# Quarter-array scores, a moved right side and later loads in a two-block kernel

## What is computed

```python
def hybrid_mixer(h, ...):
    p = jnp.einsum('bsd,de->bse', h, w_in)
    ...
    y_c = rwkv7_bidir(...)                     # the recurrence, both directions
    branch = jnp.einsum('bsnc,ncd->bsnd', ys, w_branch)
    gates = jax.nn.sigmoid(gl + b_gate)
    merged = jnp.sum(gates * branch, axis=2)
    return jnp.einsum('bsd,de->bse', merged, w_out)
...
# one step of the recurrence, 8 heads of width 64, both directions
sa = einsum('bhij,bhj->bhi', state, -kk_t)
state = state * w_t + sa * (kk_t * a_t) + v_t * k_t
y_t = einsum('bhij,bhj->bhi', state, r_t)
...
# a layer of the first block
x = layer_norm(alpha * x + mix, ln1_g[l], ln1_b[l])
hid = jnp.square(jax.nn.relu(x @ w_up[l]))
x = layer_norm(alpha * x + hid @ w_down[l], ln2_g[l], ln2_b[l])
```

## Time and profile before

| | us |
|---|---|
| median of 3 runs (2545.81 to 2548.17) | 2546.51 |
| the profiled execution | 2546.9 |
| its span, first to last instruction | 2545.1 |
| TensorE busy | 2476.9 |
| VectorE busy | 1440.0 |
| ScalarE busy | 524.4 |
| GpSimd busy | 319.5 |

### The profile page before, as it was taken

One profiled execution on the slowest core, in us unless ns is written; L12 is line 12 of the kernel. 1 busy time (PEld: TensorE's weight loads), 2 busy tenths in 40 slices (PEclk: granted clock), 3 DMA queues, 4 the chain that ended last, 5 costly groups with the idle time before them and its releaser, 6 DMA issues. The chain is left out here.

```text
span 2545.1 us, 40375 instructions
## 1 busy us (share of the span) xinstructions
PE 2476.9 (97%) x16928; PEld 1891.9 (74%) x16928; DVE 1440.0 (57%) x2688; ACT 524.4 (21%) x1233; POOL 319.5 (13%) x367
## 2 busy tenths in 40 slices
PE   8999999999999999999999999999999999999998
PEld 7887786854788778685477747888886666666997
DVE  1576655855157665563357735555334488854775
ACT  1342220100134221010014910000003243411000
POOL 2002102210100220221000000000000155410110
PEclk9999999999999999999999999999999999999999
DMA  8332125887434112597631022322222534334553
GB/s 269 116 116 69 53 85 188 297 293 246 141 117 125 59 53 85 188 301 285 241 123 67 2 67 71 95 83 75 91 87 69 165 100 134 122 104 145 167 173 108
DMA packets 253611, 341.93 MB, mean 134 GB/s; under 512 B 7252, under 2 KB 179412, under 8 KB 253304
## 3 DMA queue, kind: packets, MB, share of 16 engines
q1 hardware_dynamic: 241632, 311.71, 37.6%
q10 hardware_dynamic: 8920, 17.67, 2.2%
q0 software_dynamic: 2880, 9.96, 1.1%
HBM read 338.13 MB, written 1.19 MB: 133 GB/s over the span
## 5 line engine op out<-in xcount | busy, mean ns | idle before, releaser
L1159 PE MATMUL PS<-MEM 128*128 128x256 f32 (+1 forms) x2632 | 447.9, 332 | 2.6 <-ACT MEM L1616 1.2
L1159 PEld LDWEIGHTS PS<-MEM 128*128 128x128 f32 x2632 | 406.3, 190 | 43.8 <-issue 1.9
L415 PE MATMUL PS<-MEM 128*128 128x256 f32 x1632 | 356.8, 379 | 1.1 <-DMA MEM<-w_up 1.1
L1575 ACT ACTIVATE MEM<-PS 128x256 f32<-128x256 f32 (+3 forms) x389 | 158.8, 439 | 923.7 <-PE PS L415 223.0
L415 PEld LDWEIGHTS PS<-MEM 128*128 128x128 f32 x1632 | 308.3, 190 | 44.7 <-DMA MEM<-w_up 2.3
L470 PE MATMUL PS<-MEM 128*128 128x512 f32 x608 | 265.3, 597 | 10.9 <-DMA MEM<-w_down 6.0
L2194 DVE SCALAR_TENSOR_TENSOR MEM<-MEM 128x512 f32<-128x512 f32 x280 | 216.4, 805 | 62.7 <-DMA MEM<-ada_w 57.2
L470 PEld LDWEIGHTS PS<-MEM 128*128 128x128 f32 x608 | 115.3, 191 | 156.9 <-issue 141.5
L3139 POOL TENSOR_TENSOR MEM<-MEM 128x1 f32<-128x1 f32 (+1 forms) x34 | 21.6, 636 | 1270.3 <-DVE MEM L2140 812.8
L704 PE MATMUL PS<-MEM 128*128 128x256 f32 x768 | 180.8, 386 | 0.0
L1472 PE MATMUL PS<-MEM 128*128 128x512 f32 (+1 forms) x512 | 171.6, 488 | 0.0
(11 more groups left out here) (400 smaller groups left out, 3283.6 us busy)
## 6 DMA issues: line engine op xcount, KB each, us to landing
MEM<-w_in SPq DMA_DIRECT2D x54, 1024.0 KB, 5.4
MEM<-ada_w SPq DMA_DIRECT2D x48, 1024.0 KB, 7.3
MEM<-w_up SPq DMA_DIRECT2D x32, 1024.0 KB, 5.6
MEM<-w_down SPq DMA_DIRECT2D x32, 1024.0 KB, 5.1
MEM<-ssm_w_in SPq DMA_DIRECT2D x24, 1024.0 KB, 5.5
MEM<-ffn_gate SPq DMA_DIRECT2D x22, 1024.0 KB, 5.3
MEM<-ffn_up SPq DMA_DIRECT2D x22, 1024.0 KB, 5.3
MEM<-ffn_down SPq DMA_DIRECT2D x20, 1024.0 KB, 5.1
```

The source lines that it names most:

```text
L415: ins = pe.matmul(bank[:, 0:T], W[:, k, c * P:(c + 1) * P], XT[:, k, :], start=k == 0, stop=k == KT - 1)
L1159: ins = pe.matmul(out, left[:, k, :], right[:, k, :], start=k == 0, stop=k == 3)
L1575: act.activation(out, view(b), func, **kw).then_inc(S("bank_read_by_act"), 1)
```

## The change

It has five parts.

1. In `scores` each matmul of 128 output partitions becomes two of 64, so that each runs on one 64x64 quarter of the array. There are 16 calls a layer: 8 matmuls each in place of 4.
2. `right_first` moves from level 3 (behind its filler slot) to level 4 (before its filler slot), `right_second` from behind level 3's `level_xt` to behind level 4's filler slot. ScalarE's copy of `rh` moves along. `keys_flipped` of the next pair moves from before level 5's filler slot to behind it, and ScalarE's copy of it too.
3. In the filler's table the slot of level 2's `level_z` gets one matmul in pairs 0 and 1 (none before), and the slot `W` of pair 3 gets three (four before).
4. The waits ahead of `w_out` and `w_down` are taken out. In `wide` a wait ahead of each slab of the first half asks for as many tiles as have been used by its end: of `gated` for `w_out`, of `hid_squared` for `w_down`.
5. In layer 1 the context rows are loaded by SyncE's queue right behind the fourth slab of `w_down`'s first half, once the up products are done. ScalarE issues the five constants behind its work on the context rows at the middle of `w_down`.

```diff
@@ -57,9 +57,9 @@
 
-FILL_SLOT = {"mask": (4, 0, 0, 0), "begin": (12, 0, 0, 0), ("z", 1): (3,) * 4, ("z", 2): (0, 0, 3, 3), ("z", 3): (3,) * 4, ("z", 4): (3,) * 4, ("z", 5): (3,) * 4,
+FILL_SLOT = {"mask": (4, 0, 0, 0), "begin": (12, 0, 0, 0), ("z", 1): (3,) * 4, ("z", 2): (1, 1, 3, 3), ("z", 3): (3,) * 4, ("z", 4): (3,) * 4, ("z", 5): (3,) * 4,
              ("x", 1): (0,) * 4, ("x", 2): (0,) * 4, ("x", 3): (0,) * 4, ("x", 4): (0,) * 4, ("x", 5): (2,) * 4,
-             "W": (3, 3, 3, 4), "XO": (2, 2, 2, 4), "sa": (2, 2, 2, 4)}
+             "W": (3, 3, 3, 3), "XO": (2, 2, 2, 4), "sa": (2, 2, 2, 4)}
 
@@ -437,7 +437,7 @@
 
-            def wide(w, src, nk, keyf, nt=NT, between=None, second=None, by_token=False, midway=None, turn=None):
+            def wide(w, src, nk, keyf, nt=NT, between=None, second=None, by_token=False, midway=None, turn=None, ready=None, beside=None):
 
@@ -450,6 +450,10 @@
                         W = b_slab(w, k0, 512 * half, n)
+                        if half == 0 and s == 3 and beside:
+                            beside()
+                        if half == 0 and ready:
+                            pe.wait_ge(S(ready[0]), ready[1] + k0 + n)
                         last = k0 + n == nk
@@ -792,7 +796,8 @@
                             rhs = KR[pb:pb + 64, d, ct, c, :, :].rearrange("p a b -> p (a b)")
-                            ins = pe.matmul(banks[half][:, 256 * j:256 * j + 256], BK[pb:pb + 64, d, ct, c, part, :], rhs, start=True, stop=True)
+                            for o in (0, HB):
+                                ins = pe.matmul(banks[half][o:o + HB, 256 * j:256 * j + 256], BK[pb:pb + 64, d, ct, c, part, o:o + HB], rhs, start=True, stop=True)
                             if j == 1:
@@ -1034,12 +1039,14 @@
                                 keys_turned(g)
+                        if m == 4:
+                            right_first(gs)
+                        slot(pair, ("z", m))
+                        if m == 4:
+                            right_second(gs)
                         if m == LEVELS - 1:
...
                                 keys_flipped(g)
-                        slot(pair, ("z", m))
-                        if m == 3:
-                            right_first(gs)
                         if m == LEVELS - 1:
@@ -1048,8 +1055,6 @@
                             scores(gs[m - 1], 1)
-                        if m == 3:
-                            right_second(gs)
                         if m in (3, 4) and follow:
@@ -1080,8 +1085,7 @@
                     pass
-                pe.wait_ge(S("merged"), l + 1)
-                wide(w_out[l], lambda k, t: MRG[:, k, t * P:(t + 1) * P], KT, lambda h, t: ("wo", l, h, t), by_token=True, turn=n0 + 1)
+                wide(w_out[l], lambda k, t: MRG[:, k, t * P:(t + 1) * P], KT, lambda h, t: ("wo", l, h, t), by_token=True, turn=n0 + 1, ready=("gated", 24 * l + 16))
                 later = turn_banks(n0 + 1, 1)
@@ -1109,9 +1113,10 @@
                     channels(w_up[l], 256 * s, 256, [("up", l, 2 * s), ("up", l, 2 * s + 1)], ("act", "act"))
-                pe.wait_ge(S("hid_squared"), (DFF // P) * (l + 1))
+                up_done = len(hist)
                 wide(w_down[l], lambda k, t: HID[:, k, t * P:(t + 1) * P], DFF // P, lambda h, t: ("dn", l, h, t), between=True, by_token=True,
-                     midway=(lambda: turn_normed(0, (1,))) if l == DEPTH - 1 else None, turn=n0 + 2 if l < DEPTH - 1 else None)
+                     midway=(lambda: turn_normed(0, (1,))) if l == DEPTH - 1 else None, turn=n0 + 2 if l < DEPTH - 1 else None,
+                     ready=("hid_squared", DFF // P * l), beside=(lambda: ctx_at.append((len(slabs) - 1, up_done))) if l == DEPTH - 1 else None)
                 ada_turned(ADA_DOWN + ADA_UP)
@@ -1782,10 +1787,10 @@
                                 copy(("bkt", l, g), flat(BKT[g % 2][:, :, :]))
+                        slot(("z", m))
                         if m == LEVELS - 1 and pair < 3:
                             flipped((2 * pair + 2, 2 * pair + 3))
-                        slot(("z", m))
-                        if m == 3:
+                        if m == 4:
                             for g in gs:
@@ -1811,16 +1816,16 @@
                 if l == DEPTH - 1:
+                    squares2(0, (2, 3))
+                copy(("modrow", first), AROW, lambda b: b[:, 0:256])
+                if l == DEPTH - 1:
+                    act.wait_ge(S("x_gained"), NT * (2 * l + 2))
+                    modulated(0, (1,))
                     act.dma_start(ROT[:, :], io["rot"]).then_inc(S("const2_loaded"), 16)
...
                     act.dma_start(DIAG[:, :, :], io["diag"]).then_inc(S("const2_loaded"), 16)
-                    squares2(0, (2, 3))
-                copy(("modrow", first), AROW, lambda b: b[:, 0:256])
-                if l == DEPTH - 1:
-                    act.wait_ge(S("x_gained"), NT * (2 * l + 2))
-                    modulated(0, (1,))
                     squares2(0, (0,))
@@ -3190,7 +3195,6 @@
                 else:
-                    pool.dma_start(CTOK[:, :, :], io["ctx"].rearrange("b (t p) d -> p (b t) d", p=P)).then_inc(S("ctx_loaded"), 16)
                     for t in RMS_TILES[0][:NT]:
@@ -3268,6 +3272,9 @@
                 sp.dma_start(dst, src).then_inc(S(f"slab_loaded{s % NSLOT}"), 16)
+                if s == ctx_at[0][0]:
+                    sp.wait_ge(S("bank_filled"), ctx_at[0][1])
+                    sp.dma_start(CTOK[:, :, :], io["ctx"].rearrange("b (t p) d -> p (b t) d", p=P)).then_inc(S("ctx_loaded"), 16)
 
```

More of the change, by code:

```diff
@@ L349, in build @@
         NARROW_BANK = {"p1": 0, "p6": 1, "p7": 1, "p5": 2, "p4": 3, "p2": 4, "p3": 5}
-        narrow_at = []
+        narrow_at, ctx_at = [], []
         seven_at = []
```

## The result

The changed kernel takes 2529.65 us (median of 4 runs, 2526.40 to 2532.14), the kernel before 2546.50 beside it: 0.9932 of its time, 95% interval 0.9915 to 0.9949. So it is faster, by 16.9 us and not by 29.5, and lies 2.7 us above the forecast range. The profiled execution took 2527.41 with a span of 2525.6, that is 19.5 less than before's.

A forecast was written before the change was run, and what follows sets the result against it. TensorE, busy 97% of the span, was taken as the bound; 17.8 + 2.4 + 1.3 + 6.3 + 1.7 = 29.5 us off 2546.9 gave 2517.4, median 2517.0, range 2508.5 to 2527.

The forecast's parts named there:

- Scores as quarters: Recurrence's scores calls: four quarters run at once, so a call takes 0.90 instead of 1.21 us, 0.31 saved.
- Where the 0.31 counts: Recurrence, level by level: which calls shorten the path, with order and filler gains; 8.9 us a layer, 17.8 for two.
- The order: Recurrence, pairs 0 to 2: moved right sides save 2.8 us a layer; level 4 to 5 with flipped keys 3.5.
- The sum itself: Recurrence, per layer: level 1, level 2, levels 3 and 4, level 4 to 5, pair 3, slot W; given as 8.9.
- Z3 to X4: Recurrence, from Z of level 3 to X of level 4: 8.42 us shrinks to 7.5, 0.9 saved, three times.
- One more dip, 1.7: Layer 1's pair 3: 3.4 us at clock 0.50 expected to go with less idle time, saving 1.7 us.
- `w_out`, 2.4: Start of `w_out`: the wait of 1.2 us a layer goes, saving 2.4 us.
- `w_down`, layer 0: 0: Start wait of 1.84 us goes but comes back whole at the third slab; 0 saved, 1.8 as other bound.
- `w_down`, layer 1: 1.3 + 6.3: Start wait goes, 1.3 us; third slab's wait behind `ctx` and constants goes, 4.6, with a clock dip, 1.7.
- Quarters gain nothing: Rival on the scores: both forms fill the array, so 9 calls a layer lose 0.31 each; + 5.6, 2522.6; chance 0.12.
- The clock rival: Pair 3's dip stays and layer 0's `w_down` wait brings one of its own; + 3.4, 2520.4; chance 0.12.
- The prediction's own test: Recurrence pairs: the prediction is wrong if they shorten by less than 6 us a layer.

The follow-up runs named there:

- e1: Changed kernel with the scores written in one step over 128 rows again, not as quarters; 2528.31 us, 0.9929 of the kernel before.
- e5: Changed kernel with each 1 MB weight slab loaded during the recurrence sent as four 256 KB transfers; 2523.99 us, 0.9919 of the kernel before.
- e6: Changed kernel with scores in one step over 128 rows and the recurrence's slabs in four transfers; 2524.46 us, 0.9918 of the kernel before.
- e2: Kernel before with the scores as quarters alone; 2550.18 us, 1.0016 of the kernel before.
- e3: Kernel before with only the waits per slab in w_out and w_down and the later loads of context rows and constants; 2540.16 us, 0.9973.
- e14: Changed kernel with 32 one-column matmuls (half a block of instructions) ahead of the first projection; 2526.06 us, 0.9925 of the kernel before.
- e4: Changed kernel with 64 one-column matmuls (256 instructions, one whole block) ahead of the first projection; 2533.50 us, 0.9949 of the kernel before.
- e7: Changed kernel with each slab loaded during the recurrence sent whole and then once more; 2535.18 us, 0.9960 of the kernel before.

## Why the prediction was off

The direction and most mechanisms were right, the size was not. In the profiled execution 19.5 us came of 29.5. Of the 10.0 that are missing, 12.2 are in the recurrences (17.8 and 1.7 forecast, 7.3 found) and 1.5 in layer 1's `w_down`; 1.0 and 2.7 came where nothing was forecast. The median is 2.6 further off, for it lies 2.2 above the profiled execution and not 0.4 below. The 12.2 in turn are 8.0 us of added pauses, 1.7 for the dip that stayed, and 2.5 more.

- **Scores as quarters, "Where the 0.31 counts".** The failed step. The 0.31 a call was right (0.87 for the predicted 0.90). The sum took it for granted that TensorE always has its next instruction, and costed the doubled records at nothing beside the array's time. The quarters' share of the 17.8 was, by the prediction's own rival, 5.6 us: it came to nothing (e1, e5 against e6), and in the kernel before to a loss (e2). Between the pauses 3.4 to 4.4 of it are there, but the added pauses are 6.8 (against e1) and 8.0 (e5 against e6). The other 1 to 2 us may be calls that run into VectorE sooner, as the 0.17 at L908 shows; this is not measured.
- **The order** (right sides, flipped keys, filler): the other 12.2 of the 17.8. e1 is 11.8 us faster than e3, so this was right. Z3 to X4 took 7.57 for 7.5.
- **The sum itself.** 0.6 + 1.2 + 2.8 + 3.5 + 0.3 + 0.4 is 8.8 and not 8.9. This changes nothing that matters.
- **One more dip, 1.7.** Wrong: there is still one in the second recurrence, behind another pause. It is gone in e5. That pauses make it is likely and not shown (see below).
- **`w_out`, 2.4.** Right, 2.4 in the trace.
- **`w_down`, layer 0: 0.** 1.0 in the trace. The third slab took back 2.0, for the predicted 1.8, and a later slab was waited for 1.0 less.
- **`w_down`, layer 1: 1.3 + 6.3.** 6.1 in the trace. Of the wait for the third slab 1.34 us stayed, with the modelled end 1.5: too large by that. The clock is full there, as said.
- **The 2.7 elsewhere** are not the change's, as far as I can tell: 1.7 of it is a dip at 2250.7 that before's trace has and this one has not, and most of the rest shorter waits for `w_up` (1.1 us before, 0.3 after). That is luck of the profiled execution.
- **The rivals.** "Quarters gain nothing" was given 0.12, with 2522.6 and another reason (that both forms fill the array). Its effect came, its reason did not. The clock rival, 0.12, came by half: one dip stayed, layer 0's `w_down` has none. No case held two at once. A case in which the recurrence's instructions run short was missing, though 2.2 us of "issue" stood in the list of waits that the earlier trace rows is cut from.

The prediction's own test, pairs that shorten by less than 6 us a layer, has come true against it: 4.2 and 3.1.

## What to carry to other kernels

Count instructions as well as microseconds when a matmul is cut into smaller ones. An estimate from these traces: the 300 instructions in hand must last some 2 us until a packet starts and 2.5 until it can be used, 4.5 together. A stretch that uses them up much faster will wait, and what is saved in it can come back as pauses. Idle time put down to "issue" on a busy engine may be such a wait; see whether it stands 256 records apart. Large transfers that are not urgent are better sent in pieces in such a stretch (6.8 us here), and small matmuls kept for the places where they shorten the path.

## What the hardware showed

- TensorE's instructions come in packets of 16 KB. In the recurrences a packet starts in the mean some 2 us after record 170 of its count (3 where a 1 MB transfer is under way). The first instruction out of it runs, where TensorE paused for it, 2.2 to 3.1 us after its start, of which mostly 0.9 to 1.4 are the transfer.
- Moving the recurrence by 128 instructions changed the sum of the pauses from 10.2 and 11.7 us to 7.7 (e14), moving it by 256 left it at 11.5 (e4). Less the 1.6 us of added work e14 is 3 to 7 us faster than the changed kernel by the ratios, with intervals of some 4 us to either side.
- The recurrences of all 18 traces have 11 stretches of 3.4 us at a clock of 0.50. Each begins within 2.3 us of the end of a pause of 0.9 us or more (after 915.16, 265.23 and 844.46 in the two traces of the changed kernel); other such pauses, as two of 1.8 in e5 and one of 2.1 in e7, have none behind them. What decides is open.
